# A hybrid encoder layer with a mixture of experts: expert rows weighted by slot and added to their token's row in DRAM by indirect DMAs, in place of stores and a gather

## The chip, the cores and the metric

One core of one Trainium2 chip runs the kernel. The metric is the device time of one execution in microseconds. A core has five engines with queues of their own: PE (TensorE), DVE (VectorE), ACT (ScalarE), POOL (GpSimd) and SP (SyncE, used here only to start DMAs), and 16 DMA engines that all queues share.

## The reference

512 tokens (two requests of 256) of 1024 channels pass one encoder layer in float32. The part that matters is the expert stage at its end:

```
logit_g = h @ w_router_group + b          # 4 groups, the best one is taken
logit_e = (h @ w_router_expert + b)       # 8 experts of that group, the best two are taken
weight  = p_sel * softmax(top_logit)      # two weights for each token
y_e     = (silu(x @ w_gate[e]) * (x @ w_up[e])) @ w_down[e]        # 32 experts, 1024 -> 512 -> 1024
f       = sum over the token's two experts of weight * y_e
x       = LN(alpha * x + gate2 * f) * ln2_g + ln2_b
```

There are 512 x 2 = 1024 assignments of a token to an expert, 32 for each expert on average. Each expert has three weight matrices of 2 MiB that have to come from DRAM.

## The kernel before

**Stages.** Up to about 396 us of the profiled span come the modulation, the combined projection, the spatial gating and the pooling. From 396 to 452 us come the output projection, the first LayerNorm and the router's input. From 452 to 475 us comes the routing, while the first expert already begins. Then the 32 experts run one after the other, and the final LayerNorm ends the kernel.

**Routing** (DVE, lines 1725 to 1842). `slot_p` holds each partition's slot number. Line 1744 copies half of `h2_t[1]` out of PSUM; PE needs that copy for the last router logits. `slot_of` says which slot of an expert a token takes (1 to 64, then further rounds), `route_w` holds the two weights of each token. `positions` (line 1807) works out `pos_y`, the row of `round_y` at which each token's two results will stand. `few` says for which experts 32 rows are enough.

**One expert.** An expert takes up to CAP = 64 tokens at a time. PE runs `gate_up` (32 matmuls), `select_next` (8 matmuls that gather rows of a later expert by a 0/1 matrix), `main_transposes`, `next_columns` and `main_down` (16 matmuls). ACT does the SiLU. DVE does `hidden` (line 1915), `gate_rows` (it fills `yout[s]` with gate2's row of each slot's request, lines 1849 and 1851, by the two columns of `side`), `next_chunks` and `out_rows` (line 1933, the product with the result in bank 1). PE's `main_down` of the next expert waits for `out_rows` by the semaphore `m_sem["yo"]`. `yout` has three buffers, `gate_w` and `up_w` have three, `down_w` has two. SP starts the weight loads: `next_gate_up(e)` once `gate_up(e - 3)` is done, `next_down(e)` once `main_down(e - 2)` is done. In both cases the counts are taken from PE's semaphores `gum` and `ym`.

**Storing.** POOL waits for `yo`, reads `few` and stores 32 or 64 rows of `yout[s]` to `round_y`, in two DMAs (lines 543 and 544). `round_y` is filled with zeros before, by six DMAs of 2 MiB (line 514).

**Further rounds.** An expert with more than 64 tokens takes a branch on PE, ACT and DVE. It is taken once with these inputs. DVE's `with_further(e)` (line 1935) has this order: `further_chosen`, `hidden`, `gate_rows`, `further_columns`, `out_rows`, `further_gate`, `further_hidden`, `next_chunks`, `further_out`. PE's `with_further(e)` (line 1004) has `main_down`, `further_gate_up`, `select_next`, `further_transposes` (line 886 on `sg_hid`, it waits for `further_hidden`), `next_columns`, `further_down`.

**The end.** Expert 31 isn't stored. Its weighted 0/1 matrix `sel_last` is transposed on PE, and `last_rows` multiplies its `yout` by that straight into the sums of four token tiles. POOL waits until all stores have landed and gathers both results of each token from `round_y`: eight indirect DMAs of 128 rows of 4 KB (line 588). Tiles 0 and 1 are weighted and added on ACT and DVE (`second_scaled`, `joined`). Tiles 2 and 3 are weighted on PE, by diagonal matrices `scaling`. PE also adds the residual `res`, by the identity. Then come the sums and means (`summed`), the variance on ACT (`deviation`), and `gain`, `centred_gain`, `inverse` and `scaled_bias` on DVE. POOL adds the bias of tiles 0 and 1 (line 594). SP stores the output in the order of tiles 0, 2, 1, 3 (lines 440 and 443), with the second half of tile 3 on ACT's queue (line 1414).

Of the kernel before, what the change touches and what calls it, by code (L numbers as in the profile page):

```python
# [21 lines left out]
LAST_ROW = (NEXP + FURTHER) * CAP  # L22
ROUNDS = NEXP + FURTHER + 8
# [16 lines left out]
def hybrid_encoder(nc, x_prompt, x_sample, c_prompt, c_sample, w_mod, b_mod, w_in, b_in, w_spatial,  # L40
# [9 lines left out]
    round_y = nc.dram_tensor("round_y", (ROUNDS * CAP, D), f32).ap()  # L50

    ctx = ExitStack()
    with ctx:
# [46 lines left out]
        y_first = [at(f"y_first{i}", [128, D], f32, 2 * SLOT + (8 + 4 * i) * K) for i in range(TILES)]  # L100
        y_second = [at(f"y_second{i}", [128, D], f32, 2 * SLOT + (24 + 4 * i) * K) for i in range(TILES)]

        is_last = at("is_last", [128, TILES, CAP], f32, 8 * K)
        scaling = at("scaling", [128, 2, 2, 128], f32, 10 * K)
        sel_last = at("sel_last", [128, TILES, 2, CAP], f32, 12 * K)
        last_t = at("last_t", [128, TILES, 128], f32, 14 * K)
# [27 lines left out]
        few = at("few", [1, NEXP], i32, P0)  # L134
        n0 = at("n0", [128, NEXP], f32, P0 + 128)
        side = at("side", [128, 2, 4], f32, P0 + 256)
        w_last = at("w_last", [128, TILES], f32, P0 + 288)
# [46 lines left out]
        yout = [at(f"yout{i}", [128, 512], f32, o) for i, o in enumerate((T0 + 2048, S0 + 3584, S0 + 5632))]  # L184
        x_rows_x = at("x_rows_x", [128, 512], f32, T0)
# [33 lines left out]
        s_zero = sem("s_zero")  # L219
        s_out = sem("s_out")  # L220
# [83 lines left out]
        f_s = sem("f_s")  # L304
# [61 lines left out]
        def _(sp):  # L366
# [70 lines left out]
            for i, written, count in ((0, pool_f, 1), (2, f_o, 2), (1, pool_f, 2)):  # L437
                sp.wait_ge(written, count)
                for r, y in enumerate((y_prompt, y_sample)):
                    sp.dma_start(y[0, HALF * i:HALF * i + HALF, :], y_second[i][HALF * r:HALF * r + HALF, :]).then_inc(s_out, 16)  # L440
            sp.wait_ge(f_o, 4)
            last = TILES - 1
            sp.dma_start(y_prompt[0, HALF * last:HALF * last + HALF, :], y_second[last][0:HALF, :]).then_inc(s_out, 16)
# [4 lines left out]
        def _(pool):  # L448
# [63 lines left out]
            for k in range(LAST_ROW // 512):  # L512
                pool.wait_ge(pe_blk, 22 + 3 * k)
                pool.dma_start(round_y[512 * k:512 * k + 512, :].rearrange("(p r) (h n) -> p (r h) n", p=128, h=2), zeroes).then_inc(s_zero, 16)
            pool.wait_ge(s_zero, 16 * (LAST_ROW // 512))
# [21 lines left out]

            pool.wait_ge(dve_rt, 2)

            def store(y, turn, done, rows):  # L540

                row = turn * CAP
                pool.dma_start(round_y[bass.ds(row, rows), 0:512], y[0:rows, :]).then_inc(done, 16)  # L543
                pool.dma_start(round_y[bass.ds(row, rows), 512:1024], y[64:64 + rows, :]).then_inc(done, 16)

            def turns_of(e):
                more = pool.value_load(tab[0:1, 0, bass.ds(e, 1)], min_val=0, max_val=7)

                first = pool.value_load(tab[0:1, 1, bass.ds(e, 1)], min_val=0, max_val=FURTHER)
                return more, first  # L550

            def further_rounds(e, more, first):

                def store_further(r):
                    turn = pool.snap(e + 1 + first + r)
                    pool.wait_ge(x_sem["yo"], first + r + 2)
                    pool.sem_inc(pool_go, 1)
                    store(yout_x, turn, x_st, CAP)

                with pool.If(more > 0):  # L560
                    with pool.Fori(0, more) as r:
                        store_further(r)

            def expert(e, s):
# [5 lines left out]
                with pool.If(is_few > 0):  # L570
                    store(yout[s], turn, y_st[s], CAP // 2)
# [1559 lines left out]
```

## Time and profile before

| what | value |
|---|---|
| median of 3 runs | 976.41 us (973.46 to 977.41) |
| the profiled execution | 973.71 us |
| its span, first to last instruction | 971.8 us |
| PE busy | 914.9 us (94%) |
| DVE / ACT / POOL busy | 381.5 / 244.5 / 114.0 us |
| mean granted TensorE clock | 0.985 |
| HBM read / written | 275.81 / 21.00 MB |

The profile is one execution. Its time is 1.9 us more than its span and 2.7 us less than the median of the runs. "Busy" PE is not PE at its peak. Idle time of an engine that isn't the bottleneck costs nothing. A DMA's time "to landing" is counted from its issue.

### The profile page before, as it was taken

The numbers are of one execution on the slowest core, as the hardware profiler recorded it, in microseconds if no ns is written. First come the engines' busy times: TensorE is split into PE (matmuls) and PEld (weight loads), VectorE is DVE, ScalarE is ACT, GpSimd is POOL, SyncE is SP. The second block draws the span as 40 slices with busy tenths as digits, with TensorE's granted clock in tenths as the row PEclk, the third lists the DMA queues.
The fourth block names the chain that finished last, engine by engine and source line by source line (L and its number), as shares of the span: only waits on it lengthen the run. The fifth ranks groups of instructions, "written<-read, shape, count | busy, mean of one in ns | idle before, by whom it ended". The sixth has DMA issues, their size and how long they took to land.

```text
span 971.8 us, 11764 instructions
## 1 busy us (share of the span) xinstructions
PE 914.9 (94%) x4253; PEld 540.5 (56%) x4253; DVE 381.5 (39%) x662; ACT 244.5 (25%) x356; POOL 114.0 (12%) x173
## 2 busy tenths in 40 slices
PE   3789999999999999999999999998988999999994
PEld 2457776888888888786444344434443444444331
DVE  4522434456344236798532232222222222232235
ACT  2422233442233235445411011101100110111024
POOL 2210257100001000000000000000000000000031
PEclk9889999999999999999999999999999999999998
DMA  9984763346455822908999999999999899999973
GB/s 369 340 270 169 258 218 131 129 173 256 176 195 169 221 86 87 301 2 349 375 405 427 428 429 426 427 427 431 424 428 427 332 427 426 430 426 430 423 293 114
DMA packets 46634, 297.72 MB, mean 306 GB/s; under 512 B 4418, under 2 KB 6562, under 8 KB 30946
## 3 DMA queue, kind: packets, MB, share of 16 engines
q1 hardware_dynamic: 36352, 263.99, 67.1%
q0 software_dynamic: 9600, 31.18, 9.6%
q10 hardware_dynamic: 610, 1.66, 0.5%
q8 instruction: 37, 0.61, 0.2%
q14 instruction: 35, 0.29, 0.1%
HBM read 275.81 MB, written 21.00 MB: 305 GB/s over the span
## 4 chain that ended last, share of the span: by engine, by line
PE 84%; ACT 3%; DMA 3%; issue 3%; DVE 3%; SPq 2%; POOL 0%; DVEq 0%; POOLq 0%; ACTq 0%
PE bank L600 81%; DMA modraw<-in_w_mod 2%; PE bank L870 2%; SPq L381 2%; ACT x_rows L1073 2%; DMA y_first<-round_y,pos_y 1%; DVE wo_lo L1642 0%; PE bank L657 0%; DMA round_y<-yout 0%; ACT w_hi L1073 0%; POOL y_second L588 0%; POOL y_first L588 0%; DVE yout L1933 0%; DVE g_a L1659 0%; DVE res L1702 0%
## 5 line engine op out<-in xcount | busy, mean ns | idle before, releaser
L600 PE MATMUL bank<-up_w,x_t 128*64 128x512 f32 x512 | 225.0, 592 | 0.0
L600 PE MATMUL bank<-gate_w,x_t 128*64 128x512 f32 x512 | 225.0, 592 | 0.0
L600 PEld LDWEIGHTS bank<-gate_w,x_t 128*64 128x64 f32 x512 | 70.1, 137 | 143.1 <-issue 143.1
L600 PE MATMUL bank<-h_hi,w_hi 128*128 128x512 f32 x320 | 126.5, 395 | 1.6 <-ACT h_hi L1107 1.6
L600 PE MATMUL bank<-h_hi,w_lo 128*128 128x512 f32 x320 | 126.1, 394 | 0.0
L600 PE MATMUL bank<-down_w,hid_t 128*64 128x512 f32 x512 | 118.8, 606 | 7.6 <-issue 6.6
L600 PE MATMUL bank<-h_lo,w_hi 128*128 128x512 f32 x320 | 125.3, 399 | 0.0
L1306 ACT ACTIVATE sg_hid<-bank 64x512 f32<-64x512 f32 x33 | 19.5, 592 | 350.0 <-PE bank L600 350.0
L1915 DVE TENSOR_TENSOR sg_hid<-bank,sg_hid 64x512 f32<-64x512 f32 x32 | 22.2, 694 | 204.4 <-ACT sg_hid L1306 204.3
L1477 DVE TENSOR_TENSOR w_lo<-raw,w_hi 128x1024 fp32r<-128x1024 f32 x56 | 68.6, 1227 | 77.8 <-ACT w_hi L1073 77.8
L600 PEld LDWEIGHTS bank<-h_lo,w_hi 128*128 128x128 f32 x320 | 60.5, 189 | 25.3 <-issue 11.7
L600 PEld LDWEIGHTS bank<-down_w,hid_t 128*64 128x64 f32 x512 | 35.4, 138 | 67.8 <-issue 62.4
L543 POOL DMA_DIRECT2D round_y<-yout x31 | 16.1, 518 | 485.3 <-issue 485.3
L1073 ACT ACTIVATE w_hi<-raw 128x1024 fp32r<-128x1024 f32 x56 | 58.9, 1053 | 52.9 <-PE bank L600 51.6
L600 PEld LDWEIGHTS bank<-up_w,x_t 128*64 128x64 f32 x512 | 70.1, 137 | 0.0
L600 PEld LDWEIGHTS bank<-h_hi,w_hi 128*128 128x128 f32 x320 | 61.3, 191 | 14.1 <-ACT h_hi L1107 2.0
L600 PEld LDWEIGHTS bank<-h_hi,w_lo 128*128 128x128 f32 x320 | 61.2, 191 | 13.0
L1933 DVE TENSOR_TENSOR yout<-bank,yout 128x512 f32<-128x512 f32 x32 | 22.1, 691 | 89.8 <-PE bank L600 89.8
L600 PE MATMUL bank<-h_hi,sel 128*128 128x512 f32 x120 | 50.2, 418 | 0.0
L600 PE MATMUL bank<-a_lo,w_hi 128*128 128x512 f32 x128 | 49.9, 390 | 0.3 <-DVE w_lo L1477 0.3
L600 PE MATMUL bank<-a_hi,w_lo 128*128 128x512 f32 x128 | 49.8, 389 | 0.0
L600 PE MATMUL bank<-a_hi,w_hi 128*128 128x512 f32 x128 | 49.8, 389 | 0.0
(315 smaller groups left out, 1119.4 us busy)
## 6 DMA issues: line engine op xcount, KB each, us to landing
down_w<-in_w_exp_down SPq DMA_DIRECT2D x32, 2048.0 KB, 18.1
gate_w<-in_w_exp_gate SPq DMA_DIRECT2D x31, 2048.0 KB, 16.4
up_w<-in_w_exp_up SPq DMA_DIRECT2D x31, 2048.0 KB, 20.9
modraw<-in_w_mod SPq DMA_DIRECT2D x24, 1024.0 KB, 8.8
raw<-in_w_in SPq DMA_DIRECT2D x9, 2048.0 KB, 9.8
round_y<-zrow POOLq DMA_DIRECT2D x6, 2048.0 KB, 7.7
raw<-in_w_branch_b SPq DMA_DIRECT2D x2, 2048.0 KB, 9.4
raw<-in_w_branch_a SPq DMA_DIRECT2D x2, 2048.0 KB, 10.9
```

The costliest lines, as they stand in the source:

```text
L381: sp.dma_start(modraw0[m][:, :, :], mod_source(m)).then_inc(s_m0[m], 16)
L543: pool.dma_start(round_y[bass.ds(row, rows), 0:512], y[0:rows, :]).then_inc(done, 16)
L600: return pe.matmul(out, lhsT, rhs, start=start, stop=stop, skip_group_check=True)
L870: x = pe.transpose(bank[:, 128 * k:128 * k + 128], rows[:, 128 * k:128 * k + 128], ident)
L1073: return act.activation(out, in_, ACT.Copy, scale=scale)
L1306: act.activation(sgb[0:CAP, :], bank[0:CAP, :], ACT.Silu).then_inc(sm["silu"], 1)
L1477: dve.tensor_tensor(w_lo[par][:, :, :], raw[:, u % 2, :, 128 * (b % 4):128 * (b % 4) + 128], w_hi[par][:, :, :].bitcast(f32), ALU.subtract ...
L1915: dve.tensor_tensor(sg_hid[CAP:128, :], B[0][CAP:128, :], sg_hid[0:CAP, :], ALU.mult).then_inc(m_sem["hid"], 1)
L1933: dve.tensor_tensor(yout[s][:, :], B[1][:, :], yout[s][:, :], ALU.mult).then_inc(m_sem["yo"], 1)
```

## The change

1. `round_y` is gone, and with it five of six zero fills, `few`, `pos_y` as a gather's index, and the eight gathers. There is a DRAM tensor `added` with one row of 4 KB for each token, filled with zeros once.
2. A table `slot_table` in DRAM has two numbers for each (slot, expert): the row of `added` that belongs to the slot, less a constant, and the slot's weight. DVE computes the numbers, POOL scatters them with eight indirect DMAs of 128 pairs (8 bytes each) and reads the table back with two DMAs into `slotw`. A slot that no token has keeps zeros, and its row lies out of bounds.
3. The weight goes into `side`, so that `yout` comes out weighted.
4. For experts 0 to 29 POOL adds the 128 half rows of `yout[s]` (2 KB each) to `added`, by one indirect DMA with an addition. It waits first until the one before has landed.
5. In a further round POOL waits until the expert's own addition has landed, reads the further slots' pairs into `slotw_x`, waits for `yout_x`, adds it, and waits for that to land. DVE's `further_gate` waits for `slotw_x`.
6. Experts 30 and 31 are both added on PE, by transposed 0/1 matrices `near_t`.
7. SP loads `added` into `total[0..3]` (512 KB each) once the additions have landed. DVE adds the residual in expert 31 (`with_residual`). PE has tile 2's `total` through the identity; tiles 0, 1 and 3 get it on DVE.
8. The `ln2` rows are loaded one expert earlier. The outputs are stored in the order 0, 1, 2, 3.

```diff
             for e in (30, 31):
                 next_gate_up(e, e % 3)
                 next_down(e, e % 2)
-            for i, written, count in ((0, pool_f, 1), (2, f_o, 2), (1, pool_f, 2)):
+            for s in range(3):
+                sp.wait_ge(y_st[s], 16 * 10)
+            sp.wait_ge(x_st, 16 * allx + 16)
+            for i in range(TILES):
+                sp.dma_start(total[i][:, :], added[128 * i:128 * i + 128, :]).then_inc(f_g[i], 16)
+            for i, written, count in ((0, pool_f, 1), (1, pool_f, 2), (2, f_o, 2)):
...
+            pool.wait_ge(dve_pos, 1)
+            for j in range(2):
+                for i in range(TILES):
+                    pool.indirect_dma_start(slot_table[:, :], bass.IndirectOffsetOnAxis(pos_y[:, j, i:i + 1], 0), vals[:, j, i, :], None,
+                                            bounds_check=TOK * NEXP - 1, oob_is_err=False).then_inc(s_table, 16)
+            by_slot = slot_table[:, :].rearrange("(s e) v -> s e v", e=NEXP)
+            pool.wait_ge(s_table, 16 * 2 * TILES)
+            for c in range(2):
+                pool.dma_start(slotw[CAP * c:CAP * c + CAP, :, :], by_slot[0:CAP, :, :]).then_inc(s_slotw, 16)
+            def add_rows(rows, y, done):
+                pool.indirect_dma_start(added_halves, bass.IndirectOffsetOnAxis(rows, 0), y, None,
+                                        bounds_check=2 * TOK - 1, oob_is_err=False, compute_op=ALU.add).then_inc(done, 16)
+            def further_rounds(e):
                 more = pool.value_load(tab[0:1, 0, bass.ds(e, 1)], min_val=0, max_val=7)
                 with pool.If(more > 0):
+                    first = pool.value_load(tab[0:1, 1, bass.ds(e, 1)], min_val=0, max_val=FURTHER)
+                    near = min(e, NEXP - 3)
+                    pool.wait_ge(y_st[near % 3], 16 * (near // 3 + 1))
                     with pool.Fori(0, more) as r:
+                        ranks = pool.snap((r + 1) * CAP)
+                        for c in range(2):
+                            pool.dma_start(slotw_x[CAP * c:CAP * c + CAP, :, :], by_slot[bass.ds(ranks, CAP), e:e + 1, :]).then_inc(x_slotw, 16)
+                        pool.wait_ge(x_sem["yo"], first + r + 2)
+                        add_rows(slot_row_x[:, 0:1], yout_x[:, :], x_st)
+                        pool.wait_ge(x_st, (first + r) * 16 + 32)
             def expert(e, s):
                 pool.wait_ge(m_sem["yo"], e + 1)
+                if e:
+                    pool.wait_ge(y_st[(e - 1) % 3], 16 * ((e - 1) // 3 + 1))
+                add_rows(slot_row[:, e:e + 1], yout[s][:, :], y_st[s])
+                further_rounds(e)
...
# DVE: ahead of the copy of h2_t[1]
-            ch.did(dve.tensor_reduce(slot_p[:, :], ...))
+            link(dve.tensor_reduce(slot_p[:, :], ...))
+            link(dve.tensor_reduce(half_row[:, :], ident[:, HALF:128], AX.X, ALU.add))
+            link(dve.tensor_scalar(tok_row[:, :], slot_p[:, :], 2.0, -2.0 - NO_ROW, ALU.mult, ALU.add))
+            link(dve.scalar_tensor_tensor(out=tok_row[:, :], in0=half_row[:, :], scalar=2.0 * HALF, in1=tok_row[:, :], ...))
+            for j in range(2):
+                ch.did(dve.tensor_scalar(vals[:, j, :, 0], cst[:, C_IOTA:C_IOTA + TILES], 256.0, tok_row[:, 0:1], ALU.mult, ALU.add))
+            ch.did(dve.tensor_scalar(half_row[:, :], half_row[:, :], float(NO_ROW), None, ALU.add))
...
             def further_gate(e, turns):
-                dve.tensor_scalar(side[:, 0, 3:4], n0[:, e:e + 1], -0.5, None, ALU.is_gt).then_inc(dve_gx, 1)
+                dve.wait_ge(x_slotw, 32 * turns + 32)
+                dve.tensor_scalar(slot_row_x[:, :], slotw_x[:, :, 0], half_row[:, 0:1], None, ALU.add)
+                dve.tensor_scalar(side[:, 0, 3:4], n0[:, e:e + 1], -0.5, slotw_x[:, 0, 1:2], ALU.is_gt, ALU.mult).then_inc(dve_gx, 1)
...
# DVE, expert 0: after hidden, columns_in, next_pair and the four h2_lo
+                    dve.wait_ge(s_slotw, 32)
+                    ch.did(dve.tensor_scalar(slot_row[:, :], slotw[:, :, 0], half_row[:, 0:1], None, ALU.add))
+                    sides(e)
+                    gate_rows(e)
                     out_rows(e)
...
# DVE, expert 31: with_residual(0), (1) ahead of hidden, (2), (3) ahead of out_rows
+            def with_residual(i):
+                dve.wait_ge(f_g[i], 16)
+                dve.tensor_tensor(total[i][:, :], total[i][:, :], res[:, i, :], ALU.add).then_inc(f_b, 1)
...
# PE, the end
+            near_rows(0, 1)
             pe.wait_ge(x_sem["yo"], allx + 1)
+            near_rows(1, 0).then_inc(f_z, 1)
+            near_rows(1, 1).then_inc(f_z, 1)
+            pe.wait_ge(f_b, TILES)
+            for c in range(2):
+                mm(sums[2][c][:, :], ident, total[2][:, 512 * c:512 * c + 512], start=True, stop=False)
+            near_rows(0, 2, start=False)
+            near_rows(1, 2).then_inc(f_z, 1)
+            near_rows(0, 3)
+            near_rows(1, 3).then_inc(f_z, 1)
```

## Rows read from the trace of the kernel before

**Rows 1.** The page, parts 1 and 4: busy time, and the chain that ended last.

```profile
PE 914.9 (94%) x4253; PEld 540.5 (56%) x4253; DVE 381.5 (39%) x662; ACT 244.5 (25%) x356; POOL 114.0 (12%) x173
PE 84%; ACT 3%; DMA 3%; issue 3%; DVE 3%; SPq 2%; POOL 0%; DVEq 0%; POOLq 0%; ACTq 0%
```

**Rows 2.** Windows view: stretch, length, busy time by engine, clock, DMA share, GB/s.

```profile
470.00:480.00 10.00, 9.93 (x50) 4.02 (x48) 5.02 (x9) 6.12 (x8) 0.00 (x0) 1.00 0.78 305
480.00:741.00 261.00, 253.27 (x1171) 109.18 (x1169) 72.94 (x125) 29.45 (x56) 18.56 (x36) 0.99 1.01 425
763.00:769.00 6.00, 6.00 (x30) 2.01 (x27) 0.94 (x2) 0.27 (x1) 1.07 (x2) 1.00 0.44 153
769.00:926.00 157.00, 154.29 (x720) 64.43 (x720) 42.87 (x75) 18.00 (x35) 11.42 (x22) 1.00 1.00 423
```

**Rows 3.** Timeline of SP, 655 to 745 us: first and last of six gate loads.

```profile
656.20 0.33 SPq L397 DMA_DIRECT2D gate_w<-in_w_exp_gate  x1
...
732.38 0.33 SPq L397 DMA_DIRECT2D gate_w<-in_w_exp_gate  x1
```

**Rows 4.** Chain of waits, 655 to 770 us: start, length, what.

```profile
660.23 12.58 PE bank L600 x56
674.14 1.67 issue
675.80 14.27 PE bank L600 x56
```

**Rows 5.** DMA issues: count, KB each, median us to landing (the fifth: 760 to 775 us).

```profile
round_y<-yout POOLq DMA_DIRECT2D x30, 128.0 KB, 6.6
round_y<-yout POOLq DMA_DIRECT2D x32, 64.0 KB, 6.1
wr<-in_w_router_group POOLq DMA_DIRECT2D x1, 16.0 KB, 8.8
y_first<-round_y,pos_y POOLq DMA_INDIRECT x4, 8.0
round_y<-yout POOLq DMA_DIRECT2D x2, 128.0 KB, 2.9
```

**Rows 6.** Timeline from 761 to 771 us, the further round: start, length, engine, line.

```profile
761.86 0.69 DVE L1933 TENSOR_TENSOR yout<-bank,yout 128x512 f32<-128x512 f32 x1 [2.83 <-PE bank L600]
768.78 0.33 SPq L397 DMA_DIRECT2D gate_w<-in_w_exp_gate  x1
769.42 0.69 DVE L1881 TENSOR_TENSOR sg_hid<-bank,sg_hid 64x512 f32<-64x512 f32 x1 [5.44 <-ACT sg_hid L1306]
770.65 0.69 PE L886 MATMUL bank<-cst,sg_hid 64*128 64x64 f32 x4
```

**Rows 7.** Timeline of the router, 451 to 452 us.

```profile
451.88 0.68 DVE L1744 COPY h_t<-bank 128x512 f32<-128x512 f32 x1
```

**Rows 8.** Timeline of experts 0 and 1.

```profile
461.72 0.16 DVE L1823 TENSOR_TENSOR route_w<-route_w,q 128x4 f32<-128x4 f32 x1
491.30 0.69 PE L886 MATMUL bank<-cst,sg_hid 64*128 64x64 f32 x4
```

**Rows 9.** Timeline of the end, 926 to 966 us.

```profile
933.93 1.10 POOL L588 DMA_INDIRECT y_second<-round_y,pos_y  x1 [3.02 <-issue]
943.14 0.99 POOL L588 DMA_INDIRECT y_first<-round_y,pos_y  x1 [0.30 <-issue]
940.43 0.69 DVE L1933 TENSOR_TENSOR yout<-bank,yout 128x512 f32<-128x512 f32 x1 [3.74 <-PE bank L600]
963.74 1.41 DVE L2058 SCALAR_TENSOR_TENSOR y_second<-bank,fin,ln_bc 128x512 f32<-128x512 f32 x2
961.02 2.35 POOL L594 TENSOR_TENSOR y_second<-y_second,ln_bc 128x1024 f32<-128x1024 f32 x1 [0.92 <-DVE y_second L2045]
960.13 4.74 SPq L440 DMA_DIRECT2D out<-y_second  x6
965.18 0.63 SPq L443 DMA_DIRECT2D out<-y_second  x1
```

More of the change, by code:

```diff
@@ L582, in _ @@
[L582 to L590 removed]
+            further_rounds(NEXP - 2)
@@ L591, in _ @@
+            further_rounds(NEXP - 1)
             pool.wait_ge(s_ln2, 32)
@@ L955, in expert @@
                 select_next(e)
+                if last:
+                    near_rows(0, 0)
                 main_transposes(e)
@@ L1017, in with_further, with near_rows @@
                         further_round(e, pe.snap(first + r))
+                if e == NEXP - 1:
+                    near_rows(0, 0)
             sums = ((B[6], B[7]), (B[2], B[4]), (B[0], B[3]), (B[1], B[5]))
-            def residual(i, c):
-                mm(sums[i][c][:, :], ident, res[:, i, 512 * c:512 * c + 512], start=True, stop=False)
-            def last_rows(i):
+            def near_rows(j, i, start=True):
+                pe.wait_ge(act_sel, j + 1)
+                pe.wait_ge(m_sem["yo"], NEXP - 1 + j)
                 for c in range(2):
                     rows = slice(CAP * c, CAP * c + CAP)
-                    x = mm(sums[i][c][:, :], last_t[rows, i, :], yout[1][rows, :], start=False, stop=True)
-                x.then_inc(f_z, 1)
+                    x = mm(sums[i][c][:, :], near_t[j][rows, i, :], yout[j][rows, :], start=(j == 0 and start), stop=(j == 1))
+                return x
             pe.wait_ge(act_h2, TILES)
@@ L1339, in with_further, with expert @@
                         further_round(act.snap(first + r))
-            def expert(e, last=False):
+            def expert(e):
                 if e == 0:
@@ L1370, in expert @@
                             further_round(act.snap(first + r))
-            for e in range(NEXP - 1):
+            for e in range(NEXP):
                 expert(e)
-            expert(31, last=True)
             act.activation(fin[:, 4, 0:1], eps_col[:, :], ACT.Sqrt).then_inc(act_sq, 1)
-            def second_scaled(i):
-                act.wait_ge(f_g[i], 32)
-                copy(y_second[i][:, :], y_second[i][:, :], scale=route_w[:, 1, i:i + 1]).then_inc(f_s, 1)
             def summed(i):
@@ L1409, in _ @@
             normed(1)
-            summed(3)
             deviation(3)
@@ L2070, in _ @@
             inverse(2)
-            scaled_bias(2)
+            scaled_bias(2, [sums[2][c][:, :] for c in range(2)])
+            summed(3)
             gain(1)
-            centred_gain(3)
+            dve.wait_ge(f_x, 4)
+            ch.did(dve.scalar_tensor_tensor(out=y_out[3][:, :], in0=total[3][:, :], scalar=fin[:, 2, 3:4], in1=ln2_bc[:, 0, :], op0=ALU.add, op1=ALU.mult))
             inverse(3)
-            scaled_bias(3)
+            scaled_bias(3, [y_out[3][:, 512 * c:512 * c + 512] for c in range(2)])
             dve.br("dve_end")
```

224 lines of the change are left out of this document (94 added, 130 removed).

## Prediction

> **What bounds the kernel now.** I read the page first: PE is busy for 94% of the span, and 84% of the chain that ended last is PE [rows 1]. PE is thus the first suspect, but a share over the span hides stretches with other limits, so I cut the expert stage into windows [rows 2]. From 480 to 741 us the DMA engines are full (share 1.01, 425 GB/s) and PE is busy 253.3 of 261 us. Between 763 and 769 us the DMA share is only 0.44: all weight buffers are full. From 769 to 926 us PE is busy 154.3 of 157 us although the DMA share is 1.00.
>
> The spacing of the weight loads says which of the two sets the pace. The six gate loads from 656.20 to 732.38 us are 76.18 / 5 = 15.24 us apart [rows 3], and the chain there has waits like that of 1.67 us ahead of the down matmuls, whose weights haven't come [rows 4]. So DMA needs 15.24 us for an expert (6.29 MB of weights over 0.427 MB/us is 14.7, the rest is stores), and PE needs less. PE lives on its lead in buffers until 659 us, waits for DMA until 741 us, and from the further round at 741 to 770 us it is the bound again, since that round lets the buffers fill. It stays so to the end. Two consequences: up to 741 us what counts is DMA time and the moment at which DMA begins to be full; a stall of PE is absorbed there. After 741 us a stall of PE goes to the end whole.
>
> **The end (gain).** The first gather starts at 933.93 us and the eighth at 943.14 us, each lands about 8 us after its issue, and tile 3 waits for the last ones [rows 5, 9]. After the change the totals come by SP's plain loads, started when the addition of expert 29 has landed, about 923 us, and they are there before expert 31's product at 940.43 + 0.69 = 941.1 us [rows 9]. From that point I lay out the new order with the durations that the same operations have in the timeline of the end. PE: each `near_rows` pair 1.06 us (spacing of today's `last_rows`), the identity on tile 2 1.8 us; so the four sums are done at 942.5, 943.5, 947.4 and 949.5 us. DVE then has summed(0), summed(1) 1.5 us each, the inverses 1.0 us after ACT's second deviation (1.56 us each), to 948.4 us; centred_gain(2) 1.65, gain(0) 1.3, inverse(2) 0.9, scaled_bias(2) 1.41, summed(3) 1.5, gain(1) 1.3, the product for tile 3 1.28, inverse(3) 0.8, scaled_bias(3) 1.41. That ends at 960.4 us; today it ends at 963.74 + 1.41 = 965.15 us [rows 9]. Of this gain of 4.75 us a part is lost in SP's queue: tile 1 now stands ahead of tile 2, and POOL's addition for it ends at 956.9 + 2.35 = 959.25 us [rows 9]. Then four stores are started at 4.74 / 6, or with no wait between them some 0.67 us each, so the last one goes out at 961.95 instead of 965.18 us. **Gain 3.2 us** (2 to 4.75). The two residual additions ahead of `hidden(31)` are covered if the totals land by 932 us; if they come 2.5 us later, which the earlier `ln2` load (1 MB, 2.4 us of DMA) could do, the lower bound holds.
>
> **The further round (loss).** This is the step that I think decides. Today the further `sg_hid` is ready at 770.1 us, and PE takes it at 770.65 us [rows 6]. Now DVE's `further_gate` stands ahead of `further_hidden` and waits for `slotw_x`. POOL starts to read that only when the expert's own addition has landed. In order: `yout` is ready at 761.86 + 0.69 = 762.55; the addition starts 1.05 us later (as the first gather does behind its wait), at 763.6; it lands after 4.5 us, at 768.1. I take this between 2.9 (plain store in this very stretch, DMA half idle) and 8.0 (gather) [rows 5], nearer to the first. Then the two table reads start by 769.3, just behind the next gate and up loads at 768.78 us [rows 6], which fill the DMA again, so 6.3 us as small stores have beside weight loads [rows 5]: 775.6 us. Behind it DVE still has the two sides 0.35, the gate rows 1.3 and the hidden product 0.7 us, and PE starts 0.15 us after: 778.1 us. **Stall of PE 778.1 - 770.65 = 7.5 us.** The ends: landings of 2.9 and 2.9 give 2.4 us, landings of 8.0 and 6.6 give 11.3 us. What is queued behind the waiting DVE is everything of this and the next expert, and PE waits for that.
>
> **The clock.** After a PE wait of 1.67 us at 674.14 us the next 56 matmuls took 14.27 instead of 12.58 us [rows 4]: 1.7 us for running at the lower level for a while. A stall of 7.5 us will do the same: **+1.8 us** (0 to 3).
>
> **The router.** `slot_p` becomes a linked step, and three linked ones and three unlinked small ones come in between it and the copy of `h2_t[1]`, for which PE waits [rows 7]. A linked step of this size is 0.2 us, an unlinked one 0.08: 0.2 + 3 x 0.2 + 3 x 0.08 = 1.05 us. PE's first experts shift by that, SP's gate load at 472.5 us too, and with it the full DMA stretch, since DMA has a gap there (share 0.78) [rows 2]. **+1.05 us** (0.7 to 1.5). In exchange `dve_rt` comes earlier, which nobody needs.
>
> **The table.** `pos_y` is ready at 461.88 + 1.05 + 1.6 = 464.5 us [rows 8]; the eight scatters start from 465.5 us every 1.32 us (9.21 / 7 for the gathers) [rows 9], the last at 474.7; landed at 482; read back by about 490 us. DVE's expert 0 then has 2.4 us of work (row numbers, sides, gate rows, product) and `hidden(1)` 0.7 us. PE needs that one at 491.30 + 1.05 us [rows 8]. So it is late by 0.7 us, at most 5 us, and at that point DMA has a queue of 4 to 5 us, so it is absorbed. The scatter's own DMA time: 1024 tiny packets, as in the router weight's load, which landed in 8.8 us [rows 5]. Most lies in the gap at 470 to 480 us. **+0.5 us** (0 to 3).
>
> **The additions' DMA time.** Before: (30 x 128 + 32 x 64) KB for 31 experts [rows 5], 0.194 MB or 0.46 us each. After: 1024 rows of 4 KB over 32 experts, 0.131 MB or 0.31 us if an addition costs what a store does: 18 experts up to 741 us give -2.6 us. If it costs twice as much (it has to read the row in DRAM besides), +2.8 us. No row shows one; I take the middle, **0**. The Trainium skill (Collectives: The Full Stack, "The bandwidth ceiling: the fold count and why AG ≠ RS ≠ AR") says that the DMA engines' addition needs two reads for each write and runs at half the rate of a copy; by that rule this term is +2.8 us and the sum 3 us higher. No row of this case bears on it.
>
> What costs nothing: the zero fills taken away (PE-bound stretch), `near_rows` and the transposes of experts 30 and 31 (they lie in PE's wait for `hidden`, 1.5 us an expert), POOL's wait for the previous addition (8 us of 13.8). If an addition took over 13.8 us to land, POOL would be the bound; nothing is near that.
>
> **Sum:** -3.2 + 7.5 + 1.8 + 1.05 + 0.5 + 0 = +7.65 us. Against the profiled execution's own 973.71 us that is 981.4 us; the median of the runs is 2.7 us higher, so I predict 976.4 + 7.7 = **984.1 us**.
>
> **Rivals.** (1) Heavy additions: each costs twice a store in DMA time, and lands as late as a gather, so the stall is 11.3 us: 7.65 + 2.8 + 3.8 = +14.3, 990.7 us. For it: the addition must read and write. Against: half of the slots carry no row. Chance 0.20. (2) Not slower, by a stall that is absorbed: if the DMA queue and not PE set the pace after 769 us, the further round's wait would vanish in it like one before 741 us, and -3.2 + 1.05 + 0.5 = -1.65 gives 974.8 us. For it: DMA share 1.00 from 769 to 926 us. Against: PE has no waits there (154.3 of 157 us busy) [rows 2]. It decides if weights land later than PE wants them. Chance 0.15. (3) Light additions: landings of 2.9 us, a stall of 2.4 us, no drop of the clock, and additions as cheap as stores: -3.2 + 2.4 + 1.05 + 0.5 - 2.6 = -1.85, 974.6 us. Chance 0.15. The forecast itself has 0.50, with 980 to 989 us as its own range.
>
> **Chances.** The measurement tells about 0.5% (4.9 us) from no change, so slower means over 981.3 us: nearly three quarters of the forecast's share and all of rival 1, and a little of the rest, 0.60. Rivals 2 and 3 and the forecast's lower end make no difference, 0.33. Faster needs a rival and the larger gain at the end, 0.07. The range from 974 to 993 us leaves out the tails beyond rivals 1 and 3.
>
> **What would show it.** In the profile after: PE idle some 7 us ahead of the further round's `sg_hid` transposes, with DVE idle until the `slotw_x` reads land; a period of gate loads of still about 15.2 us before 741 us (15.1 for light, 15.4 for heavy additions); the copy of `h2_t[1]` 1 us later; some 27.5 instead of 30.7 us from the end of the last `yout` product to the span's end. I am wrong if the DVE wait in the further round is under 3 us, if the additions land after 10 us or more, or if the last product to span's end shrinks by more than 5 us.

## The result and the profile after: 17 us slower

The changed kernel takes 992.61 us (median of 4 runs, 991.20 to 996.02) against 975.62 us for the kernel before on the same chip (973.46 to 977.41): ratio 1.018, 95% interval 1.0146 to 1.0215. Forecast were +7.7 us, measured are +17.0. The range of 974 to 993 us holds the median by 0.4 us; the nearest case was rival 1 (heavy additions, 990.7 us). The profiled execution took 991.96 us, its span is 990.1 us.

The page of the changed kernel, parts 1 and 4: PE's busy time is that of before [rows 1], its share of the chain fell from 84 to 81%, and DMA's grew from 3 to 6%.

```profile
PE 915.6 (92%) x4247; PEld 539.3 (54%) x4247; DVE 385.8 (39%) x667; ACT 241.4 (24%) x351; POOL 128.5 (13%) x140
PE 81%; DMA 6%; DVE 4%; ACT 3%; issue 3%; SPq 2%; DVEq 0%; POOLq 0%; POOL 0%; ACTq 0%
```

To see where the time went, I took the start of `out_rows`' product (DVE, `yout<-bank,yout`) of some experts in both timelines:

| product of expert | before | after | shift |
|---|---|---|---|
| 18 | 740.79 | 748.99 | +8.2 |
| 19 (has the further round) | 761.86 | 768.34 | +6.5 |
| 20 | 789.53 | 807.81 | +18.3 |
| 30 | 927.26 | 945.55 | +18.3 |
| 31 | 940.43 | 963.25 | +22.8 |
| the span's end | 971.8 | 990.1 | +18.3 |

So there are four places that count: up to expert 18, the further round, expert 31, and the end behind it, which gains. From expert 18 to 19 the kernel takes back 1.7 us.

**Up to expert 18.** Windows view, as [rows 2] (columns: stretch, length, busy PE, PEld, DVE, ACT, POOL, granted clock, DMA share, GB/s). The first line is the kernel before, the others are the changed one:

```profile
460.00:466.00 6.00, 5.31 (x40) 3.45 (x42) 5.21 (x28) 2.06 (x7) 0.00 (x0) 1.00 1.00 429
460.00:466.00 6.00, 5.11 (x38) 3.41 (x38) 5.18 (x25) 1.39 (x4) 0.79 (x1) 0.53 1.00 429
470.00:480.00 10.00, 10.00 (x48) 4.02 (x44) 0.69 (x1) 5.22 (x4) 5.24 (x7) 1.00 0.41 138
480.00:741.00 261.00, 254.31 (x1153) 107.71 (x1152) 74.56 (x128) 31.55 (x58) 28.09 (x18) 0.97 1.01 418
```

The clock was granted at 0.53 from 460 to 466 us, where before it was 1.00, and the third gate load comes at 476.24 instead of 472.52 us. In the gap from 470 to 480 us the DMA share is 0.41 instead of 0.78: weights that the full stretch then has to carry. In that stretch the gate loads are 15.85 us apart (95.12 / 6) instead of 15.24 [rows 3]:

```profile
646.19 0.33 SPq L404 DMA_DIRECT2D gate_w<-in_w_exp_gate  x1
...
741.31 0.33 SPq L404 DMA_DIRECT2D gate_w<-in_w_exp_gate  x1
```

**The further round.** Timeline from 768 us, as [rows 6]. The addition of expert 19 starts 0.77 us after its product is ready at 769.03, and POOL's reads of the pairs start when it has landed. DVE waits for them for 15.74 us, and PE for DVE for 10.22:

```profile
768.34 0.69 DVE L1934 TENSOR_TENSOR yout<-bank,yout 128x512 f32<-128x512 f32 x1 [2.83 <-PE bank L605]
769.80 1.55 POOL L566 DMA_INDIRECT added<-yout,slot_row  x1 [17.79 <-DVE yout L1934]
777.60 1.18 POOL L578 DMA_DIRECT2D slotw_x<-slot_table  x2 [6.25 <-DMA added<-yout,slot_row]
784.77 0.21 DVE L1873 TENSOR_SCALAR slot_row_x<-slotw_x,half_row 128x1 uint32<-128x1 f32 x1 [15.74 <-DMA slotw_x<-slot_table]
786.57 0.69 DVE L1881 TENSOR_TENSOR sg_hid<-bank,sg_hid 64x512 f32<-64x512 f32 x1
787.41 0.71 PE L891 MATMUL bank<-cst,sg_hid 64*128 64x64 f32 x4 [10.22 <-DVE sg_hid L1881]
```

The chain of waits gives the two landings, and the 56 matmuls behind them at 13.69 instead of 12.50 us (the granted clock is 0.87 from 787 to 804 us):

```profile
769.80 6.99 DMA added<-yout,slot_row
778.18 6.56 DMA slotw_x<-slot_table
...
789.17 13.69 PE bank L605 x56
...
804.18 12.50 PE bank L605 x56
```

**Expert 31.** The chain goes through the last addition and the totals. DVE stands for them ahead of `hidden(31)`, then PE for DVE (chain and timeline):

```profile
933.77 8.71 DMA added<-yout,slot_row
942.72 10.66 DMA total<-added
```

```profile
953.47 2.38 DVE L1961 TENSOR_TENSOR total<-total,res 128x1024 f32<-128x1024 f32 x2 [6.63 <-DMA total<-added]
955.88 0.69 DVE L1916 TENSOR_TENSOR sg_hid<-bank,sg_hid 64x512 f32<-64x512 f32 x1
956.72 0.66 PE L891 MATMUL bank<-cst,sg_hid 64*128 64x64 f32 x4 [2.77 <-DVE sg_hid L1916]
957.86 5.35 PE L605 MATMUL bank<-down_w,hid_t 128*64 128x512 f32 x16 [0.47 <-ACT hid_t L1079]
963.25 0.69 DVE L1934 TENSOR_TENSOR yout<-bank,yout 128x512 f32<-128x512 f32 x1 [2.98 <-PE bank L605]
```

The 16 down matmuls take 5.35 us (the granted clock is 0.81 from 955 to 964 us); those of expert 30 took 3.65. Behind the last product's end at 963.94 us the kernel needs 26.2 us more; before it was 30.7.

### The profile page after: what moved, and what is told of

The parts are those of the page before. It is cut to its first block, busy times and chain, and to the rows that moved or that the text cites. A ratio compares the mean times of both kernels' runs of the same rounds, so it can differ in the third digit from the quotient of the medians.

```text
span 990.1 us, 11392 instructions
## 1 busy us (share of the span) xinstructions
PE 915.6 (92%) x4247; PEld 539.3 (54%) x4247; DVE 385.8 (39%) x667; ACT 241.4 (24%) x351; POOL 128.5 (13%) x140
## 4 chain that ended last, share of the span: by engine, by line
PE 81%; DMA 6%; DVE 4%; ACT 3%; issue 3%; SPq 2%; DVEq 0%; POOLq 0%; POOL 0%; ACTq 0%
PE bank L605 78%; DMA modraw<-in_w_mod 2%; PE bank L875 2%; SPq L388 2%; ACT x_rows L1079 2%; DMA added<-yout,slot_row 2%; DMA total<-added 1%; DMA slotw_x<-slot_table 1%; DVE wo_lo L1642 0%; PE bank L662 0%; DVE y_out L2059 0%; DVE yout L1934 0%; ACT w_hi L1079 0%; PE bank L891 0%; DVE y_out L2072 0%
## 5 line engine op out<-in xcount | busy, mean ns | idle before, releaser
L605 PE MATMUL bank<-down_w,hid_t 128*64 128x512 f32 x512 | 125.2, 634 | 7.4 <-issue 6.3
L566 POOL DMA_INDIRECT added<-yout,slot_row x30 | 46.7, 1556 | 384.9 <-DVE yout L1934 384.9
L605 PEld LDWEIGHTS bank<-h_lo,w_hi 128*128 128x128 f32 x320 | 60.4, 189 | 25.1 <-issue 11.7
```

The lines of the kernel that those rows point to most:

```text
L566: pool.indirect_dma_start(added_halves, bass.IndirectOffsetOnAxis(rows, 0), y, None, bounds_check=2 * TOK - 1, oob_is_err=False, compute_o ...
L605: return pe.matmul(out, lhsT, rhs, start=start, stop=stop, skip_group_check=True)
```

## Experiments

Each label is followed by its median, the ratio to the kernel before of the same chip job and its 95% interval. "Measured" gives the difference of medians to the changed kernel, where nothing else is said; times of products come from the profiled runs. The spacing of two experts is the time from one's product to the other's, the last spacing that from expert 30's to expert 31's. Some kernels spread by 8 to 10 us from run to run (`a_plain` from 973.0 to 982.4), and they ran on different chips, so differences of medians are good to 2 or 3 us at best; places are read from the traces.

**Pairs read ahead** (`a_pairs`: 986.07 us, 1.010, 1.0072 to 1.0129).

```diff
 def expert(e, s):
+    # if this expert has a further round: read its pairs into slotw_x here
     pool.wait_ge(m_sem["yo"], e + 1)
```

> The changed kernel, but POOL reads the further slots' pairs (slotw_x) ahead of the wait for the expert's product, not behind the landing of its addition. Theory (the further round's stall is the chain addition lands, then pairs are read): slotw_x is there some 13 us before DVE wants it, PE's 10.3 us wait ahead of the further round's sg_hid transposes goes, and with it the 1.5 us of lower clock behind it: 11 to 12 us less in all, and less again if the end's 2.9 us wait shrinks. Rival (PE is paced by the weights after the further round, so the stall was absorbed): the wait goes but the time falls by under 4 us, since waits for weights take its place before 926 us.

Measured: -6.5 us. At its place the wait is gone: `slot_row_x` (line 1891 of this kernel) is computed right behind the product, and from expert 19's product to expert 20's it takes 27.66 us as before the change (27.67), where the changed kernel takes 39.47. That is the whole 11.8 us. The span of this profile is only 5.2 us shorter, for two reasons. Expert 19's product comes 4.5 us later than in the changed kernel (772.79 against 768.34), ahead of the place. Behind it DVE stands longer for the totals, and the last spacing is 19.44 us instead of 17.70.

```profile
772.79 0.69 DVE L1952 TENSOR_TENSOR yout<-bank,yout 128x512 f32<-128x512 f32 x1 [2.83 <-PE bank L623]
773.40 0.20 DVE L1891 TENSOR_SCALAR slot_row_x<-slotw_x,half_row 128x1 uint32<-128x1 f32 x1
...
947.49 2.38 DVE L1979 TENSOR_TENSOR total<-total,res 128x1024 f32<-128x1024 f32 x2 [8.01 <-DMA total<-added]
```

**Router's operations behind the last copy** (`a_router`: 992.67 us, 1.018, 1.0152 to 1.0209).

```diff
-            # the seven small operations, ahead of the copy of h2_t[1]
             dve.tensor_copy(h2_t[1][:, 4:8, :], ...)
+            # the seven small operations, behind it
```

> The changed kernel, but the six small DVE operations for the slots' rows stand behind the copy of h2_t[1], in DVE's wait for the last router logits. Theory (1.0 us of DVE delay makes PE idle 1.16 us, and the clock then falls to 0.5 to 0.6 of full speed at 460 to 466 us, 2.8 us more): the first expert's gate matmuls start at 465.2 instead of 468.9 us, the clock stays 1.00, and the whole kernel is 3 to 4 us faster. Rival (the start of the experts is absorbed by the weights' pace up to 741 us): the start moves by 3.7 us and the time by under 1 us.

Measured: nothing. The copy comes at 451.00 us, PE no longer stands for it, yet the clock still fell (0.63 of full from 460 to 466 us). Expert 18's product comes 2.6 us earlier all the same and expert 19's 2.3. Two waits take this back: from expert 19's product to expert 20's it takes 41.19 us instead of 39.47 (the addition lands after 7.53 instead of 6.99 us, and the 56 matmuls take 14.95 instead of 13.69), and the last spacing is 18.72 instead of 17.70.

**Residual behind hidden(31)** (`a_resid`: 989.44 us, 1.0141, 1.0112 to 1.0171).

```diff
-                        with_residual(0); with_residual(1)
                     hidden(e)
                     gate_rows(e)
                     next_chunks(e)
+                        with_residual(0); with_residual(1); with_residual(2)
                     out_rows(e)
# with_residual(3) behind summed(1)
```

> The changed kernel, but the residual additions of tiles 0 to 2 stand behind hidden(31) and gate_rows(31), that of tile 3 behind summed(1). Theory (DVE waits for total[0] ahead of hidden(31), so PE waits 2.8 us and runs at a lower clock in the last down matmuls, 5.35 instead of 3.65 us): 3 to 5 us faster. Rival (the totals' landing at 953.4 us is what the end waits for in either order): no change, within 1 us.

Measured: -3.2 us; the last spacing is 13.10 us, as before the change (13.17).

**Write instead of add** (`a_plain`: 980.86 us, 1.0026, 0.9995 to 1.0058).

```diff
-    bounds_check=2 * TOK - 1, oob_is_err=False, compute_op=ALU.add)
+    bounds_check=2 * TOK - 1, oob_is_err=False)
```

> The changed kernel with the indirect DMAs for the experts' rows as plain writes to the same rows, without the addition; what each token's sum should hold is left out (only the last writer stays). Theory (an addition takes the DMA engines about twice as long as a write, 0.65 against 0.3 to 0.45 us an expert): landing falls from 10.8 to about 8 us, the yout product at 749.0 us comes some 3 to 5 us earlier, PE's further wait shrinks by the shorter landing (2 to 3 us): 5 to 8 us faster in all. Rival (128 descriptors with an index are what costs, added or not): landing and time the same within 1.5 us.

Measured: -11.8 us by the medians (by the ratios 15), more than expected. Expert 18's product is at 741.67 us (-7.3), and as the last addition lands sooner, the last spacing is 13.10 us (-4.6). The wait in the further round stays (39.35 us from product to product), where 2 to 3 us less were expected.

**All three edits** (`a_three`: 976.30 us, 1.0002, 0.9980 to 1.0024).

> The changed kernel with the pairs read ahead, the router's operations moved behind the last h_t copy and the residual behind hidden(31); the additions by DMA stay. Theory (the losses add up): 992.6 - 6.5 (pairs) - 3.2 (residual) - 0 (router) = 982.9; with the totals' wait gone, more than the 6.5 of the pairs can show, since in the run with the pairs alone the last spacing grew from 17.70 to 19.44 us: down to 981. Rival (the time that the pairs give back is taken by later weights, as in that run): 985 to 988, no faster than the pairs alone. Against the kernel with the scatter by choice the difference is what the accumulate costs, less its 3 us for the extra loads.

Measured: -16.3 us, where the three alone sum to 9.7 by the medians. The change now costs nothing that can be measured, with every addition still in it. The products of the profiled runs show where the difference lies (`a_pairs_resid` and `a_pairs_router` are described below):

| kernel | product of 19 | 19 to 20 | 30 to 31 | span |
|---|---|---|---|---|
| changed | 768.34 | 39.47 | 17.70 | 990.1 |
| `a_pairs` | 772.79 | 27.66 | 19.44 | 984.9 |
| `a_resid` | 771.65 | 37.68 | 13.10 | 987.2 |
| `a_router` | 766.01 | 41.19 | 18.72 | 990.7 |
| `a_pairs_resid` | 773.55 | 27.66 | 13.12 | 979.1 |
| `a_pairs_router` | 766.85 | 27.67 | 19.50 | 978.9 |
| `a_three` | 770.67 | 27.66 | 13.10 | 976.3 |

At its own place the pairs' edit gives 11.8 us alone and in company. The residual's gives 4.6 alone and 6.3 beside the pairs', and the two make 16.4 us of the changed kernel's spacings. Up to expert 19, where neither edit changes anything that PE waits for, the single profiles differ: `a_pairs` and `a_resid` came 4.5 and 3.3 us later than the changed kernel, which is most of what they lack. Whether that is chance isn't shown. That losses hid one another is shown for 1.7 us of the last spacing and for the router's 2.3 us, no more.

**All three, and a write for each choice** (`b_choice`: 974.35 us, 0.9988, 0.9972 to 1.0004).

```diff
-    added = nc.dram_tensor("added", (TOK, D), f32).ap()
+    added = nc.dram_tensor("added", (2 * TOK, D), f32).ap()   # a second choice's row lies TOK rows further
-    ..., oob_is_err=False, compute_op=ALU.add)
+    ..., oob_is_err=False)
+                sp.dma_start(y_out[i][:, :], added[TOK + 128 * i:TOK + 128 * i + 128, :]).then_inc(f_g[i], 16)
+                # DVE: total[i] += y_out[i], then += res
```

> The changed kernel with the pairs of a further round read ahead of POOL's wait, the router's seven operations behind the last h_t copy, the residual behind hidden(31), and no addition by DMA: the scatter writes a first choice's row into one tensor and a second choice's into another, and at the end both are loaded and added on VectorE (the result is the reference's). Theory (the accumulate in the DMA, the read of the pairs in series, and the totals' wait ahead of hidden(31) are the three losses, and they add up nearly): 992.6 - 11.8 (as the run without the accumulate) - 6.5 (pairs) - 1 (of the residual's 3.2, since the run without the accumulate had 13.10 us at the last spacing already) + 3 (2 MB more to load and four more VectorE additions of 2.4 us, partly beside PE) = 976, range 971 to 982. Rival (the losses hide one another, since the weight queue sets the pace once the stalls are gone): 981 to 986.

Measured: inside the expected range, 1.2 us below the kernel before and not told from it. Expert 18's product is at 739.80 us. But the last spacing is 16.76 us: DVE's six additions (7.3 us) stand ahead of the last product.

**One matmul more for the clock** (`a_keep`: 994.33 us, 1.0195, 1.0166 to 1.0225).

```diff
+                    if i == TILES - 1 and kc == 4:
+                        mm(B[7][:, :], ident, cst[:, 0:512])
                     x = mm(B[6][...], h2_t[i % 2][:, kc, :], wr[:, kc, :], ...)
```

> The changed kernel with one more 128x512 matmul (into a bank not in use, 0.5 to 0.9 us) between the two halves of the last logits, so that PE does not stand 1.16 us at 453.5 for h_t. Theory A (that standstill is what brings the clock down to 0.5-0.6 of full in 460 to 466): the clock stays at 1.00 there, the third gate load issues at 473 to 473.5 instead of 476.24, and the time falls by about 3: 989.5. Theory B (the clock falls in this stretch whatever PE does in that gap, as in the run with the router's operations moved, where PE did not stand and the clock was 0.71 in 456 to 460 and 0.50 in 460 to 464): the low stretch is still there and the time is within 1 us of 992.6.

This run tests neither theory. The extra matmul stands behind PE's wait for the copy, and not ahead of it, so PE stood 1.17 us before it (the line is this matmul, in two instructions). The clock was 0.50 from 460 to 466 us, and the time is 1.7 us above the changed kernel's.

```profile
452.93 1.12 PE L605 MATMUL bank<-cst 128*128 128x512 f32 x2 [1.17 <-DVE h_t L1752]
```

What speaks against the standstill as the only cause is `a_router`, where PE did not stand and the clock was 0.50 from 460 to 464 us.

**Each addition twice** (`a_twice`: 1048.86 us, 1.0764, 1.0734 to 1.0795).

```diff
                 add_rows(slot_row[:, e:e + 1], yout[s][:, :], y_st[s])
+                # the same rows once more, into a scratch tensor, same semaphore
```

> The changed kernel with each main round's addition issued twice: once more into a scratch tensor of the same size (zeroed with the first), same rows; the further rounds once. Theory (an addition costs DMA time beyond its bytes, and the weight queue pays it): the run without the accumulate was 7.3 us earlier at expert 18's product, over 19 experts; a second addition costs that 7.3 and its writes besides, about 3 us of the queue's 261: expert 18's product at 759 to 761 instead of 748.99, the end 14 to 20 later, 1007 to 1013. Rival (the 7.3 us come from when an addition lands and the waits on that, not from the DMA engines' time): the second addition shows mainly as a later landing, and the end is 0 to 6 later, 993 to 999.

Both missed: +56 us. The timeline shows another mechanism. POOL waits for the landing of the last pair of additions before it starts the next, and with about 14 us of that wait and 3.8 us of starting, the chain takes some 17.5 us an expert, where PE needs 13.83. Then DVE waits to refill `yout`:

```profile
644.45 0.49 DVE L1851 TENSOR_SCALAR yout<-gate_half,side 128x512 f32<-128x512 f32 x1 [10.23 <-DMA added<-yout,slot_row]
645.24 1.90 POOL L568 DMA_INDIRECT added<-yout,slot_row  x1 [14.87 <-DMA added<-yout,slot_row]
647.45 1.55 POOL L592 DMA_INDIRECT added<-yout,slot_row  x1 [0.30 <-issue]
```

In the changed kernel itself POOL's 30 additions are all released by `yout` (384.9 of 384.9 us of its idle time ahead of them), none by a landing: there the chain is no limit, but its landings of 10.8 us (median) are not far from one. In `a_three` four additions in a row (504.85 to 542.13 us) were started by the landing of the one before, 11.8 to 13.3 us after it had started, against PE's 13.83.

**Two of the three edits** (`a_pairs_resid`: 978.23 us, 1.0031, 1.0003 to 1.0059; `a_pairs_router`: 981.21 us, 1.0070, 1.0047 to 1.0093).

> The changed kernel with the pairs of a further round read ahead and the residual behind hidden(31); the router's operations stay where the change has them. The two edits alone gave 6.5 and 3.2, the three together 16.3. Theory (the residual's wait is worth more once the pairs' wait is gone: with the pairs alone VectorE stood 8.01 us for the totals ahead of hidden(31) and the last spacing of the products was 19.44 instead of 13.1 us): 986.1 - 6.3 = 979.8, last spacing 13.1; the router then is worth the 3.5 left. Rival (the router's edit gives nothing in any company, as alone): 975.5 to 977.5, as with all three.

> The changed kernel with the pairs of a further round read ahead and the router's seven operations behind the last h_t copy; the residual stays ahead of hidden(31). Theory (as for the run with pairs and residual; the router's edit keeps the clock up in 452 to 466, which gave 3 to 4 us earlier third gate loads in the run with all three): 986.1 - 3.5 = 982.6, last spacing 19 to 20 us, the wait for the totals still 7 to 8. Rival (the router's edit gives nothing, alone or in company, and the clock in that stretch comes and goes by itself): 985.5 to 987.

The first theory holds in the main, for both. By the medians the residual's place is worth 3.2 us alone and 7.8 with the pairs mended, the pairs 6.5 alone and 11.2 with the residual mended, and the router's edit 0 alone, 4.9 with the pairs, 1.9 with both. By the ratios the last two are 2.9 and 2.8 us, so the router's edit gives some 2 to 5 us in company.

**The router's operations in the kernel before** (`b_router`: 977.22 us, 1.0026, 1.0011 to 1.0041).

```diff
+            # the seven small operations of the change, results unused
             dve.wait_ge(pe_rt, 2 * TILES)
             dve.wait_ge(pe_lg, 2)
             dve.tensor_copy(h2_t[1][:, 4:8, :], ...)
```

> The kernel before with the seven small VectorE operations of the change put ahead of its last h_t copy (their results are not used): the router term alone, without anything else of the change. Prediction's theory: the copy 1.05 us later and the time too, 976.6. Rival A (the standstill brings the clock down in 460 to 466, 2.8 us more): third gate load at 476, time 978 to 980. Rival B (the weight queue is the limit of the stretch behind, so a late start of the experts is taken up by it): the time within 0.5 us of 975.6.

Measured: +2.5 us (1.1 to 4.0 by the interval), between the prediction's theory and rival A; PE stood 1.17 us for the copy, the clock was 0.79 of full from 452 to 460 us, and the third gate load came at 475.72 us.

**Writes by choice, DVE's additions reordered** (`b_choice2`: 971.78 us, 0.9974, 0.9955 to 0.9993).

> The kernel with the scatter by choice (two totals, no accumulate), with the third token tile's two VectorE additions moved behind the last expert's product; they stood before it and held it back: the last spacing was 16.76 us instead of 13.1, the product at 942.95 with PE's products done at 939.2 or so. VectorE stands 2.26 us behind the product for PE, which covers the 2.4. Theory: the product 2.4 earlier and the time too, 974.35 - 2.4 = 972, 0.4% below the kernel before. Rival (PE's matmul of the third total, or the squares on ScalarE, take the 2.4 back): 974 to 975.

Measured as expected. This version is faster than the kernel before by 0.26% (0.07 to 0.45), a small gain whose interval is just clear of none. The last spacing is 14.37 us.

**What an addition costs the DMA engines** (`t_plain`: 970.10 us, 0.9946, 0.9924 to 0.9967; `t_write`: 987.54 us, 1.0153, 1.0116 to 1.0190; `t_add`: 1003.32 us, 1.0291, 1.0255 to 1.0328). All three start from `a_three`. In `t_plain`, as in `a_plain`, the sums are left out, and only the last writer of a row stays.

```diff
# t_plain: add_rows without compute_op=ALU.add
# t_add, behind add_rows(...) of each main round; t_write the same without compute_op
+                if e > 1:
+                    pool.wait_ge(y_two[e % 2], 16 * (e // 2))
+                pool.indirect_dma_start(scratch[e % 2] half rows, slot_row[:, e:e + 1], yout[s][:, :], ..., compute_op=ALU.add)
```

> The changed kernel with pairs, router and residual mended, and its indirect DMAs write instead of adding (the sums are left out). Against the run with the three edits and the additions (976.3; expert 18's product at 749.88, last product 949.2) this is the price of the accumulate alone. Theory (it costs DMA time that the weights lose): expert 18's product at 740 to 743, the time 8 lower, 968. Rival (the time is made up behind 741, where the weights have slack): expert 18's product earlier, but the time only 0 to 3 lower, 973 to 976.

> The three-edit kernel with a second addition of each main round's rows into one of two scratch tensors in turn, so that it waits for nothing that is not long landed. If an addition costs the weight queue its time on the engines: that time is 11.7 us for 18 additions in the trace of the changed kernel (4.5% of 261 us), so expert 18's product comes 11 to 13 us later than 749.88, and the end as much: 986 to 990. Rival (only landings and chains cost, or POOL's wait for them sets the pace again): VectorE then waits for landed additions as in the doubled run, and the end is over 1000; or nothing: 976 to 980.

> As the run with the second addition, but the second indirect DMA of each main round is a plain write of the same rows into the scratch tensors. By the engines' time (2.2% of 261 us for 18 plain writes in the run without the accumulate, 5.7 us): expert 18's product 5 to 6 us later than 749.88, the time 981 to 983, and 5 to 7 below the run with the second addition. Rival (the number of scattered rows is what costs, not the accumulate): the same time as the run with the second addition, within 2 us.

The DMA view of a stretch gives the software queue's packets, MB and share of the 16 engines' time. From 480 to 741 us, the kernel before, the changed one, and `t_plain`:

```profile
q0 software_dynamic: 1408, 3.41, 3.3%
```

```profile
q0 software_dynamic: 2529, 1.94, 4.5%
```

```profile
q0 software_dynamic: 1504, 2.06, 2.2%
```

Of 261 us these are 8.6, 11.7 and 5.7 us (`a_three` has 4.5% too). The same rows cost twice the engines' time when added, and 1.36 times that of the old stores, which moved more bytes. From 480 to 925 us, `t_plain`, `a_three`, `t_write` and `t_add`:

```profile
q0 software_dynamic: 2608, 3.73, 2.3%
```

```profile
q0 software_dynamic: 4455, 3.63, 4.9%
```

```profile
q0 software_dynamic: 6672, 6.92, 6.8%
```

```profile
q0 software_dynamic: 8098, 6.65, 9.0%
```

Of 445 us: 10.2, 21.8, 30.3 and 40.0 us; the kernels' medians are 970.1, 976.3, 987.5 and 1003.3. The accumulate (11.6 us of the engines for 31 rounds, 0.37 each) costs this kernel 6.2 us, between the 8 of the theory and the 0 to 3 of the rival, and expert 18's product comes 6.8 us earlier without it. A second write (8.5 us) costs 11.2 and a second addition (18.2) 27.0; by the spans of the profiled runs the three are 6.6, 6.5 and 27.6, so the write's price is uncertain (its runs lie between 984.6 and 994.0). The expected times of `t_write` and `t_add` were too low: they counted only up to 741 us, and in `t_add` 10.3 of the 27.6 us come between experts 20 and 30. At expert 18 `t_add` is 16.4 us later (11 to 13 expected) and `t_write` 2.5 (5 to 6 expected), so the engines' share gives the size and not the place. In `t_add` no DVE idle time is ended by a landed addition, so `a_twice`'s chain is absent; weights come late, now also after the further round (from 850 to 975 us the load of `up_w` has 22.4% of the chain of waits).

## Why the prediction was wrong

The sum by places, forecast and measured in the spans: up to expert 18 +1.55 and +8.2 us (1.7 of them given back by expert 19), the further round +9.3 and +11.8, expert 31 and the end -3.2 and 0. The step that failed is the price of an addition: its DMA time was put at nothing, its landing in the further round at 4.5 us where it took 6.99, and at the end the totals behind it were taken to be there in time.

- **The additions' DMA time, forecast 0** ("No row shows one; I take the middle"): this step failed. The software queue's time on the engines up to 741 us grew by 3.1 us over the old stores', just above my upper bound of 2.8. Against plain writes of the same rows, which are cheaper than the old stores, the accumulate is worth 6.2 us (`t_plain` against `a_three`) to 11.8 (`a_plain` against the change, with the totals' wait that hangs on it). The rule of the Trainium skill (Collectives: The Full Stack, "The bandwidth ceiling: the fold count and why AG ≠ RS ≠ AR") that I weighed and set aside, stated there for collectives, was borne out in direction and size: a factor of 2.05 between adding and writing the same rows (11.7 against 5.7 us). A gate period of 15.4 us was forecast for heavy additions; measured were 15.85. The sign that I had named against me, additions that land after 10 us or more, was there: 10.8 us in the median, 10.9 for those after 782 us. Rival 1 had this mechanism right and missed the clock ahead of expert 0 and the totals' wait.
- **The further round, 7.5 us**: the mechanism was right, step for step; mis-sized was the addition's landing, 6.99 us where I had put 4.5. The reads landed after 6.6 (6.3 forecast), and 0.77 us lay ahead of the addition (1.05 forecast). PE's wait was 10.22 us, inside my 2.4 to 11.3. With the clock behind it (1.5 us; forecast 1.8) this place costs 11.8 us, and removing it gave back just that much at its place (`a_pairs`).
- **Rival 2, a stall that is absorbed**, did not occur at the place: the shift of +18.3 us stood from expert 20 to expert 30.
- **The end, -3.2 us**: behind the last product the gain was larger, 4.5 us. But the condition that I named, totals there by 932 us (950.3 with the shift of 18.3), did not hold: they were there at 953.47, since expert 29's addition took 8.71 us to land and the loads 10.66. The wait and the lower clock behind it cost 4.5 us at expert 31. The end gave nothing in sum, where 3.2 were forecast. With writes in place of additions (`a_plain`), or with the residual behind `hidden(31)` (`a_resid`), these 4.6 us are gone. In my list of the end the terms behind 948.4 us add up to 11.55, which ends at 959.95 and not at 960.4 us; the gain of 3.2 rests on the stores and stays.
- **The router, 1.05 us**: the copy came 0.9 us later, as said. What I missed is the clock: the 32 matmuls of the first expert's selection took 6.48 us at 0.53 of the full clock, about the lower of its two levels (1.2 GHz), and 3.67 before. In the kernel before the term costs 2.5 us by itself. In the changed kernel moving it gave nothing: the clock fell all the same, and the two waits behind expert 19 took back the 2.3 us gained there.
- **The table, 0.5 us**: in the changed kernel DVE took it at 486.54 us without a wait. That is luck in part, since the lower clock had delayed the first expert: in `a_three`, where the clock stayed up, DVE waited 4.56 us ahead of `slot_row` and PE then 0.47 us for `hidden(1)`, near the 0.7 us that the prediction has.
- **POOL's wait for the addition before, "nothing is near that"**: too sure. Where additions waited for one another (`a_three`), they came 11.8 to 13.3 us apart, under PE's 13.83 by 0.5 to 2 us.

Of the span's +18.3 us the places thus account for 8.2 - 1.7 + 11.8 + 4.5 - 4.5. The 8.2 us at expert 18 can be taken as 3.7 us of a later third gate load and 3.1 us of the additions by the engines' share, an estimate; 1.4 us are not explained, and over the eight kernels with one addition an expert, with 3.1 taken for each, that rest ranges from -0.5 to +4.9 us. That is left open, as is what brings the clock down between 452 and 470 us: in all eight profiles in which PE stood 1.16 or 1.17 us for the copy it fell (`a_keep` among them), but also in five of the nine others. `a_router` takes only the standstill away, and the clock fell, so the standstill isn't needed for it; whether it adds to it is not shown.

## What to carry to other kernels

Here an addition in DRAM cost the DMA engines twice a write of the same rows and landed 2.7 us later. Before such a change, look first at everything that waits for its landing (a read behind it, the next addition, the final load), and take the reads that don't depend on it out of that line. Where two addends are all there are, write them to two places and add them on an idle engine. Read what an edit is worth at its own place, not from the total alone: here three edits gave 6.5, 3.2 and 0 us alone and 16.3 together, while the places of the first two gave 11.8 and at least 4.6 each time. An edit that shows nothing alone is not yet shown to be free, since a wait further on can take its gain back. And check in the trace that an edit meant to fill a standstill really stands ahead of the wait.

## What was not expected of the hardware

- A 128-row addition took 10.8 us from issue to landing (median of 18 beside weight loads), a plain indirect write of the same rows 8.1 us.
- An addition into DRAM made 2529 packets where the write of the same rows made 1504, for about the same 2 MB.
- The granted clock fell to about half for some microseconds with PE busy 5.1 of 6 us, in kernels that have one more wait of 1.16 us in that place or none (`t_plain` and `t_add`, 0.51 and 0.52).
